# Last attention of a four-block transformer kernel: the fifth maximum ahead of four halves of output weights, the fifth scores half a column block later

## The chip, the cores and the metric

The kernel runs on one core of a Trainium2 chip. The time is that of the device for one launch, in microseconds. The kernel before has a median of 1317.13 us in three runs (1316.91 to 1317.64).

## The reference

One sequence of 256 tokens, width 1024, float32 throughout, passes through four blocks and two final norms: stick-breaking attention with an MLP, retention with an MLP, gated linear attention with a convolutional FFN, and, last, a sparse attention (NSA) with an FFN. The change lies in this last attention. Cut to it:

```
kv = (rmsnorm(x, g_kv) @ w_kv)                  # keys and values of three branches, 4 heads of 64
k_cmp, v_cmp = compress(kv[0]), compress(kv[1])  # 15 blocks of 32 tokens, a small MLP with gelu
q     = (rmsnorm(x, g) @ w_in)[:, :1024]         # 16 heads of 64;  gates = sigmoid(the last 48 columns)
p_cmp = masked_softmax(q @ k_cmp.T * scale);  o_cmp = p_cmp @ v_cmp
q_rot = rope(q)
o_sel = masked_softmax(q_rot @ k_sel.T * scale) @ v_sel
o_win = masked_softmax(q_rot @ k_win.T * scale) @ v_win
x     = x + (gates[0]*o_cmp + gates[1]*o_sel + gates[2]*o_win) @ w_o
```

With 256 tokens every block is selected, so the two uncompressed branches are plain causal attention.

## The kernel before

All 212 weight pieces of 128 x 2048 pass through one pipeline, each in two halves of 128 x 1024. SyncE loads a half into a ring of four raw buffers (`stream`), ScalarE rounds it to w_hi (`hi_half`, L1352), VectorE takes the rest as w_lo (`lo_half`, L1938), and TensorE multiplies with three products, hi·hi, hi·lo and lo·hi (`mm3`, L592 to L594). The raw buffer of half q comes free when VectorE has done half q - 4:

```
                if turn is not None or q >= RAW:
                    sp.wait_ge(lo_ready, plus(q - RAW + 1, turn, RAW))
```

w_hi and w_lo hold four pieces each; `refill(g)` on ScalarE waits for TensorE to be done with piece g and then copies both halves of piece g + 4. The halves come in the same order on every engine. So the DMAs of the two halves of piece G_NSA+16 wait for VectorE's two halves of G_NSA+14.

The order on each engine is that of the code, and every engine works its instructions in that order; between the engines stand semaphores. The last attention begins at piece G_NSA = 161. Its queries come in column blocks of 256 (`transposed`: two parts j of 128 columns, eight k of three matmuls each), pieces G_NSA+6 and G_NSA+11 to G_NSA+13. Into these blocks other steps are put: `mid` between the two parts, `late` ahead of k = 4 of the second. The output weights are pieces G_NSA+14 to G_NSA+17.

The attention has 16 steps `it`, two for each pair of heads (selected and window branch). For each: scores on TensorE (`ns_qk`, L1210), mask and maximum on VectorE (`ns_scores`, L2545), exponential on ScalarE (`ns_exp`, L1795), coefficient on VectorE (`ns_coef`, L2556 and L2561), the multiplication on GpSimd (L534), transposes on TensorE (`ns_t`, L1223), copies, and the product with the values (`ns_pv`, L1235 and L1241), whose result ScalarE copies (`ns_hi`, L1812 and L1814) and VectorE splits (`ns_lo`, L2565). ns_qk(it) waits for the maximum of the step before. "The fifth scores" are ns_qk(4).

The compressed branch comes in two parts c: `ns_cmp_kv` (L1163, L1168), `ns_cmp_values` (L2505), scores on TensorE (`ns_cmp_qk`, L1181), which wait for the maximum 5 + c, `ns_cmp_scores` on VectorE (L2518 to L2522), `ns_cmp_exp` on ScalarE (L1784), `ns_cmp_p` on VectorE (L2529 to L2533), the transpose on TensorE (`ns_cmp_t`, L1190), which is the `late` step of the column block G_NSA+13. Queries are scaled by `ns_queries` (L1985) when their block is done, swapped by a matmul (`ns_swap`, L1133) and rotated by `ns_rope` (L2460, L2467) and, on GpSimd, L526.

What ScalarE does around the change, in its order:

```
            ns_cmp_keys()
            ns_exp(4)
            refill(G_NSA + 12)
            ns_cmp_exp(0)
            ns_exp(5)
            ns_cmp_copy(0)
            ns_hi(0)
            ns_cmp_exp(1)
            ns_hi(1)
            ns_copy(4)
```

Here refill(G_NSA + 12) copies both halves of piece G_NSA+16. ns_t(4) on TensorE waits, by nsa_o_copied, for the first copy of ns_hi(1).

Of the kernel before, what the change touches and what calls it, by code (L numbers as in the profile page):

```python
# [72 lines left out]
G_NSA = 161  # L73
# [6 lines left out]
def build(nc, ws, small, narrow, tables, decay, rows, x_in, out):  # L80
    from contextlib import ExitStack
    ctx = ExitStack()
    with ctx:
# [461 lines left out]
        def _(pe):  # L545
# [25 lines left out]
            def x_tiles(n, k, t=1):  # L571
                if k % 2 == 0:
                    pe.wait_ge(xT_lo, xt_at(n, t, k // 2))
# [12 lines left out]
            def split(g, e):  # L586

                pe.wait_ge(lo_ready, 2 * g + e + 1)

            def mm3(o, lh, ll, rh, rl, start, stop):  # L590

                mm(o, lh, rh, start=start, stop=False, skip_group_check=True)  # L592
                mm(o, lh, rl, start=False, stop=False, skip_group_check=True)  # L593
                return mm(o, ll, rh, start=False, stop=stop, skip_group_check=True)  # L594

            def transposed(g, b, first=None, mid=None, src=(x_hi, x_lo), late=None):

                s = g % RING
                for j in range(2):
                    if j == 1 and mid is not None:  # L600
                        mid()
                    for k in range(KT):
                        if (j, k) == (1, 4) and late is not None:
                            late()
                        if j == 0 and k % 4 == 0:
                            split(g, k // 4)
                        if first is not None and j == 0:
                            x_tiles(first, k)
                        c = k * 256 + j * P
                        r = mm3(ps[:, b, j * T:(j + 1) * T], w_hi[:, s, c:c + P], w_lo[:, s, c:c + P],  # L610
                                src[0][:, k, :], src[1][:, k, :], k == 0, k == KT - 1)
                r.then_inc(done, 1)
# [511 lines left out]
            mixed = (y_hi, y_lo)  # L1124

            def ns_swap(i):

                if i < 2:
                    pe.wait_ge(nsa_kv, 3 + i)
                else:  # L1130
                    pe.wait_ge(nsa_q_in, i - 1)
                b, src = (4 + i, ns_k[:, i, :, :]) if i < 2 else (i % 2, ns_q[:, 2 * (i - 2):2 * (i - 2) + 2, :])
                mm(ps[:, b, :], swap, src, start=True, stop=True).then_inc(nsa_swapped, 1)  # L1133
# [25 lines left out]
            def ns_cmp_kv():  # L1159

                pe.wait_ge(nsa_gelu, 3)
                for c in range(2):
                    r = mm(ps[:, 2, 384:448], sm[:, S_W2K + c * P:S_W2K + (c + 1) * P], ns_h[:, 2, c, :],  # L1163
                           start=c == 0, stop=c == 1)
                r.then_inc(nsa_cmp_kv, 1)
                for g in range(2):
                    for c in range(2):
                        r = mm(ps[:, 3, 384 + g * 64:384 + (g + 1) * 64], ns_hv[:, g, c, :],  # L1168
                               sm[:, S_W2V + c * 64:S_W2V + (c + 1) * 64], start=c == 0, stop=c == 1)
                r.then_inc(nsa_cmp_kv, 1)  # L1170
# [22 lines left out]
            def ns_qk(it):  # L1193


                pr, br = it // 2, it % 2
                if it < 2:
                    pe.wait_ge(nsa_kd_other, it + 1)
                    pe.wait_ge(nsa_sin, 2)
                if it >= 5:  # L1200
                    pe.wait_ge(nsa_cmp_scores_copied, 1 if it < 6 else 2)
                if it >= 6:
                    pe.wait_ge(nsa_cmp_pT_copied, 1 if it < 10 else 2)
                pe.wait_ge(nsa_roped, pr // 2 + 1)
                if it:
                    pe.wait_ge(nsa_max, it)
                for t in range(TT):
                    for i in range(2):
                        v = slice(64 * i, 64 * i + 64)
                        r = mm(ps[:, 4 + i, P * t:P * (2 * t + 1)], ns_qr[v, pr, t * P:(t + 1) * P],  # L1210
                               ns_kd[v, br, pr // 2, 0:P * (t + 1)], start=t == 0, stop=True, skip_group_check=True)
                r.then_inc(nsa_scores, 1)

            def ns_t(it):
                pe.wait_ge(nsa_p, it + 1)
                if it:
                    pe.wait_ge(nsa_pT_copied, it)
                    pe.wait_ge(nsa_pT_copied2, it)
                if it >= 4:
                    pe.wait_ge(nsa_o_copied, 2 * max(it // 2, 2) - 1)  # L1220
                for i in range(2):
                    for j in range(3):
                        r = nc.tensor.transpose(ps[:, 6 + i, j * P:(j + 1) * P],  # L1223
                                                ns_s[it][:, i, j * P:(j + 1) * P], ident)
                r.then_inc(nsa_pT, 1)
# [64 lines left out]
            pe.wait_ge(nsa_gate_in, 1)  # L1290
            transposed(G_NSA + 11, 1, src=mixed, mid=lambda: (ns_hidden_t(), ns_t(2)))
            ns_t(3)
            transposed(G_NSA + 12, 0, src=mixed, mid=lambda: (ns_swap(3), ns_cmp_kv(), ns_qk(4)))
            ns_cmp_qk(0)
            ns_swap(4)
            ns_qk(5)
# [624 lines left out]
        def _(dve):  # L1921
# [13 lines left out]
            def lo_half(q):  # L1935
                g, v = q // 2, slice((q % 2) * HALF, (q % 2 + 1) * HALF)
                dve.wait_ge(hi_ready, q + 1)
                V.tensor_tensor(w_lo[:, g % RING, v], ring[:, q % RAW, :], w_hi[:, g % RING, v].bitcast(F32),  # L1938
                                ALU.subtract).then_inc(lo_ready, 1)

            def lo(g):
                lo_half(2 * g)
                lo_half(2 * g + 1)

            def refill(g):
                if g + RING < G_END:
                    lo(g + RING)
# [285 lines left out]
            for u in range(8):  # L2233
                dve.wait_ge(small_in, RET_SMALL + u + 1)
                b, src = rt_pair[u % 4][0], rt_small[:, u % 2, :].rearrange("p (a t) -> p a t", t=T)
# [198 lines left out]
            late = ffn(0)  # L2434
# [15 lines left out]
            def ns_queries(u):  # L2450
                dve.wait_ge(done, G_NSA + (7 if u == 0 else 11 + u))
                scaled(ns_q[:, 2 * u:2 * u + 2, :], ps[:, u % 2, :], scale, 0.125).then_inc(nsa_q_in, 1)
# [3 lines left out]
            def ns_sin(i):  # L2456
                dve.wait_ge(nsa_swapped, i + 1)
                if i >= 2:
                    dve.wait_ge(nsa_roped, i - 2)
                V.tensor_tensor(ns_t2[i == 1], ps[:, 4 + i if i < 2 else i % 2, :].rearrange("p (a t) -> p a t", t=T), rsin,  # L2460
                                ALU.mult).then_inc(nsa_sin, 1)
# [7 lines left out]
            def ns_rope(u):  # L2469
                ns_sin(2 + u)  # L2470
                ns_roped(u)
# [42 lines left out]
            def ns_cmp_scores(c):  # L2514
                s, m, _ = ns_cmp(c)
                dve.wait_ge(nsa_cmp_scores, c + 1)
                add = tab[:, C_CADD:C_CADD + TT * CMP].rearrange("p (t n) -> p t n", n=CMP)
                V.tensor_tensor(s, ns_cmp_at.rearrange("p t (h n) -> p t h n", n=CMP),  # L2518
                                add.unsqueeze(2).broadcast_to([P, TT, 8, CMP]), ALU.add).then_inc(nsa_cmp_scores_copied, 1)
                dve.wait_ge(nsa_cmp_scores_copied, c + 1)  # L2520
                link(V.tensor_reduce(m, s, AX.X, ALU.max))
                V.tensor_tensor(s, s, m.unsqueeze(3).broadcast_to([P, TT, 8, CMP]), ALU.subtract).then_inc(nsa_cmp_shifted, 1)  # L2522
# [27 lines left out]
            def ns_coef(it):  # L2550

                dve.wait_ge(nsa_exp, it + 1)
                if it >= 4:
                    dve.wait_ge(nsa_p, it - 3)
                l, f = ns_l[:, it % 4, :, :], ns_f[:, it % 4, :, :]
                link(V.reciprocal(f, l))  # L2556
                pr, br = it // 2, it % 2
                if it == 0:
                    dve.wait_ge(nsa_gate_in, 1)
                g = ns_gate[:, :, 16 * (br + 1) + 2 * pr:16 * (br + 1) + 2 * pr + 2].rearrange("p t h -> p h t")  # L2560
                V.tensor_tensor(f, f, g, ALU.mult).then_inc(nsa_coef, 1)  # L2561
# [64 lines left out]
            ns_gelu()  # L2626
            ns_copy(3)
            ns_rope(1)
            refill(G_NSA + 10)
            ns_cmp_values()  # L2630
            ns_scores(4)
            lo_half(2 * (G_NSA + 15))
            ns_queries(2)
            ns_cmp_scores(0)
            ns_coef(4)
            ns_scores(5)
            ns_cmp_p(0)
            ns_rope(2)
            ns_coef(5)
            lo_half(2 * (G_NSA + 15) + 1)  # L2640
            ns_queries(3)
            lo_half(2 * (G_NSA + 16))
            ns_lo(0)
            ns_sin(5)
            ns_cmp_scores(1)
            ns_scores(6)
            ns_lo(1)
# [244 lines left out]
```

## Time and profile before

| | |
|---|---|
| median of three runs | 1317.13 us |
| profiled execution: time | 1316.63 us |
| profiled execution: span | 1314.9 us |
| TensorE busy | 1305.7 us, 99% of the span |
| VectorE busy | 981.3 us, 75% |
| ScalarE busy | 758.8 us, 58% |
| GpSimd busy | 125.4 us, 10% |
| granted clock of TensorE, mean | 0.999 |

The profile comes from one execution. Its times are counted from the span's start. The engines' names in it are PE (TensorE), DVE (VectorE), ACT (ScalarE), POOL (GpSimd) and SP (SyncE). A row of a timeline gives start, duration, engine, line and operation; in square brackets stands how long the engine was idle ahead of it and which instruction ended that. Instructions of an engine overlap a little, so that one can start about 0.1 us before the one ahead of it ends, and matmuls overlap by more.

### The profile page before, as it was taken

How to read it: one execution, taken by the hardware profiler on the slowest of the kernel's cores; microseconds unless marked ns; L12 is line 12 of the kernel's file. 1: busy time of each engine (PE TensorE's matmuls, PEld its weight loads, DVE VectorE, ACT ScalarE, POOL GpSimd, SP SyncE). 2: the span in 40 equal slices, each digit the busy share in tenths (PEclk: the TensorE clock that was granted, in tenths of full speed). 3: DMA queues.
4: the chain of work that ended last, by engine and by line, in shares of the span. 5: the costliest groups of instructions: out<-in, count | busy, mean ns of one | idle time of the engine just before them, and what ended most of it. 6: DMA issues, size and time to landing. Idle time of an engine off the chain costs nothing.

```text
span 1314.9 us, 20491 instructions
## 1 busy us (share of the span) xinstructions
PE 1305.7 (99%) x7401; PEld 1118.4 (85%) x7401; DVE 981.3 (75%) x1518; ACT 758.8 (58%) x1231; POOL 125.4 (10%) x123
## 2 busy tenths in 40 slices
PE   9999999999999999999999999999999999999998
PEld 8888888888888888888889888888889878888886
DVE  5957765657846657665668768998868986899886
ACT  6655554536445446454566357666658756766663
POOL 0101000001600100000001310000003234000000
PEclk9999999999999999999999999999999999999999
DMA  7536656565654465656555445565546422466651
GB/s 263 194 129 207 224 186 206 175 205 163 198 194 133 155 225 159 223 172 210 170 162 201 128 162 170 192 207 189 190 155 210 139 71 81 161 192 196 200 193 53
DMA packets 64022, 231.61 MB, mean 176 GB/s; under 512 B 7104, under 2 KB 7488, under 8 KB 63936
## 3 DMA queue, kind: packets, MB, share of 16 engines
q1 hardware_dynamic: 62208, 224.42, 52.3%
q10 hardware_dynamic: 1728, 6.00, 1.3%
q8 instruction: 59, 0.97, 0.3%
q14 instruction: 27, 0.22, 0.1%
HBM read 229.34 MB, written 1.05 MB: 175 GB/s over the span
## 4 chain that ended last, share of the span: by engine, by line
PE 97%; DVE 2%; issue 1%; ACT 0%; POOL 0%; POOLq 0%; DVEq 0%
PE ps L645 25%; PE ps L592 17%; PE ps L594 17%; PE ps L593 17%; PE ps L653 13%; PE ps L564 1%; PE ps L1049 1%; PE ps L1241 1%; PE ps L1223 1%; PE ps L1210 1%; DVE w_lo L1938 1%; PE ps L884 0%; PE ps L873 0%; PE ps L1133 0%; PE ps L1235 0%
## 5 line engine op out<-in xcount | busy, mean ns | idle before, releaser
L1938 DVE TENSOR_TENSOR w_lo<-ring,w_hi 128x1024 fp32r<-128x1024 f32 x423 | 518.5, 1257 | 127.5 <-ACT w_hi L1352 126.9
L1352 ACT ACTIVATE w_hi<-ring 128x1024 fp32r<-128x1024 f32 x423 | 431.4, 1054 | 145.0 <-PE ps L594 116.3
L645 PE MATMUL ps<-x_both,w_hi 128*128 128x512 f32 x1408 | 340.1, 392 | 0.0
L645 PEld LDWEIGHTS ps<-x_both,w_hi 128*128 128x128 f32 x1408 | 258.5, 188 | 52.7 <-issue 1.6
L592 PE MATMUL ps<-w_hi,y_hi 128*128 128x512 f32 (+1 forms) x564 | 221.1, 392 | 0.0
L593 PE MATMUL ps<-w_lo,y_hi 128*128 128x512 f32 (+1 forms) x564 | 219.0, 388 | 0.0
L594 PE MATMUL ps<-w_hi,y_lo 128*128 128x512 f32 (+1 forms) x564 | 218.9, 388 | 0.0
L653 PEld LDWEIGHTS ps<-x_both,w_lo 128*128 128x128 f32 x1408 | 182.1, 191 | 7.9
L653 PE MATMUL ps<-x_both,w_lo 128*128 128x256 f32 x1408 | 184.5, 283 | 0.0
L594 PEld LDWEIGHTS ps<-w_hi,y_lo 128*128 128x128 f32 x564 | 105.9, 188 | 22.2
L592 PEld LDWEIGHTS ps<-w_hi,y_hi 128*128 128x128 f32 x564 | 106.1, 188 | 21.5 <-issue 0.8
L593 PEld LDWEIGHTS ps<-w_lo,y_hi 128*128 128x128 f32 x564 | 106.1, 188 | 19.9
L592 PE MATMUL ps<-w_hi,x_both 128*128 128x512 f32 (+1 forms) x300 | 118.6, 395 | 0.4 <-DVE w_lo L1938 0.4
L594 PE MATMUL ps<-w_hi,x_both 128*128 128x512 f32 (+1 forms) x300 | 113.8, 379 | 0.0
L593 PE MATMUL ps<-w_lo,x_both 128*128 128x512 f32 (+1 forms) x300 | 113.4, 378 | 0.0
L438 POOL TENSOR_TENSOR stat<-stat,power 128x1 f32<-128x1 f32 x20 | 10.9, 547 | 853.0 <-DVE stat L1933 675.6
L1458 ACT ACTIVATE arena<-arena,sm 128x256 f32<-128x256 f32 x88 | 48.2, 595 | 38.3 <-DVE arena L2095 38.3
L1374 ACT ACTIVATE x_both<-ps,sm 128x128 fp32r<-128x128 f32 x128 | 35.8, 374 | 59.1 <-PE ps L564 59.0
L592 PEld LDWEIGHTS ps<-w_hi,x_both 128*128 128x128 f32 (+1 forms) x300 | 54.6, 182 | 14.0 <-issue 4.0
L594 PEld LDWEIGHTS ps<-w_hi,x_both 128*128 128x128 f32 (+1 forms) x300 | 54.5, 182 | 11.0
L593 PEld LDWEIGHTS ps<-w_lo,x_both 128*128 128x128 f32 (+1 forms) x300 | 54.7, 182 | 9.7 <-issue 0.5
L592 PE MATMUL ps<-x_both,w_hi 128*128 128x256 f32 x192 | 55.0, 286 | 0.0
(262 smaller groups left out, 1521.9 us busy)
## 6 DMA issues: line engine op xcount, KB each, us to landing
ring<-ws SPq DMA_DIRECT2D x424, 512.0 KB, 4.8
tab<-tables ACTq DMA_DIRECT2D x3, 572.0 KB, 5.8
rowg<-rows ACTq DMA_DIRECT2D x3, 512.0 KB, 6.4
h<-x SPq DMA_DIRECT2D x4, 256.0 KB, 6.1
arena<-decay ACTq DMA_DIRECT2D x1, 768.0 KB, 10.1
sm<-small ACTq DMA_DIRECT2D x1, 642.0 KB, 6.4
arena<-narrow ACTq DMA_DIRECT2D x1, 512.0 KB, 6.7
out<-arena SPq DMA_DIRECT2D x2, 256.0 KB, 2.2
```

What stands on the lines that cost most here:

```text
L564: r = nc.tensor.transpose(ps[:, base + k // 2, t * T + (k % 2) * P:t * T + (k % 2 + 1) * P], h[:, t, k * P:(k + 1) * P], ident)
L592: mm(o, lh, rh, start=start, stop=False, skip_group_check=True)
L593: mm(o, lh, rl, start=False, stop=False, skip_group_check=True)
L594: return mm(o, ll, rh, start=False, stop=stop, skip_group_check=True)
L645: mm(ps[:, b + j, :], w_hi[:, s, c:c + P], x_both[:, k, :, :], start=k == 0, stop=False, skip_group_check=True)
L653: r = mm(ps[:, b + j, T:2 * T], w_lo[:, s, c:c + P], x_hi[:, k, :], start=False, stop=k == KT - 1, skip_group_check=True)
L1049: r = mm(o, keys, q, start=True, stop=True, skip_group_check=True)
L1210: r = mm(ps[:, 4 + i, P * t:P * (2 * t + 1)], ns_qr[v, pr, t * P:(t + 1) * P], ns_kd[v, br, pr // 2, 0:P * (t + 1)], start=t == 0, stop=Tr ...
L1352: A(w_hi[:, q // 2 % RING, c:c + HALF], ring[:, q % RAW, :], ACT.Copy).then_inc(hi_ready, 1)
L1374: r = A(dst[:, k, t * P:(t + 1) * P], ps[:, base + b, t * T + (k % 2) * P:t * T + (k % 2 + 1) * P], ACT.Copy, scale=gain(n, k))
L1458: r = A(conv[:, u % 2, e, :], conv_in[:, u % 2, e, :], ACT.Identity, scale=par(u, 4 + e), bias=par(u, 6 + e))
L1938: V.tensor_tensor(w_lo[:, g % RING, v], ring[:, q % RAW, :], w_hi[:, g % RING, v].bitcast(F32), ALU.subtract).then_inc(lo_ready, 1)
```

## The change

On VectorE the two halves of piece G_NSA+14 (until now refill(G_NSA + 10)) leave their place ahead of ns_cmp_values; they stand on either side of ns_cmp_scores(0). The two halves of G_NSA+15 and the first of G_NSA+16 move back likewise. On TensorE ns_qk(4) moves from `mid` to `late` of the column block G_NSA+12. ScalarE, GpSimd and SyncE keep their order.

```diff
-            transposed(G_NSA + 12, 0, src=mixed, mid=lambda: (ns_swap(3), ns_cmp_kv(), ns_qk(4)))
+            transposed(G_NSA + 12, 0, src=mixed, mid=lambda: (ns_swap(3), ns_cmp_kv()), late=lambda: ns_qk(4))
...
             ns_rope(1)
-            refill(G_NSA + 10)
             ns_cmp_values()
             ns_scores(4)
-            lo_half(2 * (G_NSA + 15))
             ns_queries(2)
+            lo_half(2 * (G_NSA + 14))
             ns_cmp_scores(0)
+            lo_half(2 * (G_NSA + 14) + 1)
             ns_coef(4)
             ns_scores(5)
             ns_cmp_p(0)
             ns_rope(2)
             ns_coef(5)
+            lo_half(2 * (G_NSA + 15))
+            ns_queries(3)
             lo_half(2 * (G_NSA + 15) + 1)
-            ns_queries(3)
-            lo_half(2 * (G_NSA + 16))
             ns_lo(0)
             ns_sin(5)
+            lo_half(2 * (G_NSA + 16))
             ns_cmp_scores(1)
```

VectorE from the end of ns_rope(1) (L2467) on, before: L1938 are halves of weights, L2505 ns_cmp_values, L2545 on arena<-ps,tab the fifth maximum.

```order
 L2467 TENSOR_TENSOR arena<-arena 128x512
-L1938 TENSOR_TENSOR w_lo<-ring,w_hi 128x1024 x2
 L2505 TENSOR_TENSOR arena<-ps,tab 128x512 x2
 L2545 ISA arena<-ps,tab 128x128
```

The two halves ahead of the maximum are gone from there. Right behind the maximum, up to the coefficient of the fifth step (L2556), VectorE changes as follows; L1985 is ns_queries(2), L2518 to L2522 ns_cmp_scores(0).

```order
-L1938 TENSOR_TENSOR w_lo<-ring,w_hi 128x1024
-L1985 SCALAR_TENSOR_TENSOR arena<-ps,arena 128x512
+L1985 SCALAR_TENSOR_TENSOR arena<-ps,arena 128x512
+L1938 TENSOR_TENSOR w_lo<-ring,w_hi 128x1024
 L2518 TENSOR_TENSOR arena<-ps,tab 128x2x128
 L2521 TENSOR_REDUCE arena<-arena 128x2x8
 L2522 TENSOR_TENSOR arena<-arena 128x2x128
+L1938 TENSOR_TENSOR w_lo<-ring,w_hi 128x1024
 L2556 RECIPROCAL arena<-arena 128x4
```

Where one half of G_NSA+15 stood, there are now the two of G_NSA+14, one ahead of the compressed scores and one behind them. Ahead of the second part of the compressed scores, a half stands between ns_sin(5) (L2460) and ns_cmp_scores(1) that stood ahead of ns_lo(0) (L2565) before.

```order
 L2460 TENSOR_TENSOR arena<-ps,tab 128x512
+L1938 TENSOR_TENSOR w_lo<-ring,w_hi 128x1024
 L2518 TENSOR_TENSOR arena<-ps,tab 128x2x128
 L2521 TENSOR_REDUCE arena<-arena 128x2x8
 L2522 TENSOR_TENSOR arena<-arena 128x2x128
```

The halves ahead of this point are the same five as before.

## Rows read from the trace of the kernel before

**Rows 1.** The page's first part: busy us, share, instructions.

```profile
PE 1305.7 (99%) x7401; PEld 1118.4 (85%) x7401; DVE 981.3 (75%) x1518; ACT 758.8 (58%) x1231; POOL 125.4 (10%) x123
```

**Rows 2.** Timeline of TensorE: start, us, instruction, idle before.

```profile
1048.40 0.93 PE L1210 MATMUL ps<-arena 64*128 64x128 f32 x8 [0.22 <-DVE arena L2467]
1049.26 0.39 PE L592 MATMUL ps<-y_hi,w_hi 128*128 128x256 f32 x1
...
1052.11 0.28 PE L594 MATMUL ps<-y_hi,w_lo 128*128 128x256 f32 x1
1053.07 1.94 PE L1181 MATMUL ps<-arena 128*128 128x32 f32 x16 [0.68 <-DVE arena L2545]
...
1055.88 0.93 PE L1210 MATMUL ps<-arena 64*128 64x128 f32 x8
...
1061.15 0.38 PE L1190 MATMUL ps<-sm,arena 128*128 128x128 f32 x2
...
1069.55 0.93 PE L1210 MATMUL ps<-arena 64*128 64x128 f32 x8
1070.40 0.87 PE L1223 MATMUL ps<-sm,arena 128*128 128x128 f32 x6
```

**Rows 3.** Timeline of VectorE, 1048 to 1076.

```profile
1048.27 2.35 DVE L1938 TENSOR_TENSOR w_lo<-ring,w_hi 128x1024 fp32r<-128x1024 f32 x2
...
1051.74 0.28 DVE L2545 CUSTOM_DVE_ANT_0 arena<-ps,tab 128x128 f32<-128x128 f32 x1
...
1052.84 0.08 DVE L2545 DVE_READ_ACCUMULATOR2_ANT arena<- 128x1 f32 x1
...
1053.98 0.68 DVE L1985 SCALAR_TENSOR_TENSOR arena<-ps,arena 128x512 f32<-128x512 f32 x1
1055.05 0.42 DVE L2518 TENSOR_TENSOR arena<-ps,tab 128x256 f32<-128x256 f32 x1 [0.39 <-PE ps L1181]
...
1060.24 0.68 DVE L2460 TENSOR_TENSOR arena<-ps,tab 128x512 f32<-128x512 f32 x1
...
1061.86 1.22 DVE L1938 TENSOR_TENSOR w_lo<-ring,w_hi 128x1024 fp32r<-128x1024 f32 x1
...
1063.61 2.02 DVE L1938 TENSOR_TENSOR w_lo<-ring,w_hi 128x1024 fp32r<-128x1024 f32 x1
...
1067.66 0.42 DVE L2518 TENSOR_TENSOR arena<-ps,tab 128x256 f32<-128x256 f32 x1
...
1073.99 0.41 DVE L2529 TENSOR_REDUCE arena<-arena 128x16 f32<-128x256 f32 x1
...
1075.14 0.42 DVE L2533 TENSOR_TENSOR arena<-arena 128x256 f32<-128x256 f32 x1
```

**Rows 4.** Timeline of ScalarE, 1054 to 1070.

```profile
1054.73 1.99 ACT L1352 ACTIVATE w_hi<-ring 128x1024 fp32r<-128x1024 f32 x2
...
1069.04 0.42 ACT L1784 ACTIVATE arena<-arena 128x256 f32<-128x256 f32 x1 [3.29 <-DVE arena L2522]
1069.66 0.38 ACT L1812 ACTIVATE arena<-ps 128x256 f32<-128x256 f32 x1 [0.21 <-PE ps L1241]
```

**Rows 5.** DMAs into the ring, 1049 to 1053; last row: 1063 to 1068.

```profile
L403 SPq DMA_DIRECT2D ring<-ws x2: 333/333/333, 1049.7 to 1050.8; - x2
...
DMA to landing us min/median/max: 3.7/4.3/4.8
...
DMA to landing us min/median/max: 3.5/3.6/3.7
```

**Rows 6.** Timeline of GpSimd, 1062.

```profile
1062.02 2.52 POOL L534 TENSOR_TENSOR arena<-arena 128x256 f32<-128x256 f32 x2 [2.39 <-DVE arena L2561]
```

**Rows 7.** Windows: TensorE busy, granted clock, DMA share, GB/s.

```profile
1308.00:1309.00 1.00, 0.46 (x4) 1.00 0.11 43
...
1311.00:1312.00 1.00, 0.00 (x0) 1.00 0.00 0
1312.00:1313.00 1.00, 0.00 (x0) 0.56 0.40 144
```

## The prediction

> **What bounds the kernel now.** I read the page first. Its busy line has TensorE occupied for 99% of the span [rows 1], so the kernel is one long file of matmuls and time is lost or won only where that file stops. I then asked for the waits of TensorE in the last attention (1015 to 1105 us) and found three short ones; the timeline of TensorE shows the two that the change touches [rows 2]. The fifth scores, ns_qk(4) at L1210, start at 1048.40 after 0.22 us of idleness, released by VectorE's rotated queries. The first compressed scores, ns_cmp_qk(0) at L1181, start at 1053.07 after 0.68 us, released by the fifth maximum (L2545). Third, the timeline of VectorE says why that maximum is late: two halves of output weights (L1938 x2, 2.35 us at 1048.27) stand ahead of it, so ns_scores(4) runs only from 1051.74 to 1052.92 [rows 3]. Fourth, and this decides for me, ScalarE: its two weight copies of piece G_NSA+16 (L1352 x2 at 1054.73) stand directly ahead of the exponential of the compressed scores (L1784), and they find their data already there [rows 4]. That data comes by DMAs which SyncE may issue only when VectorE has finished the two halves of G_NSA+14, because lo_ready frees the raw buffer four halves on. In the kernel before they were issued at 1049.7 and 1050.8 and landed 3.7 to 4.8 us later [rows 5], by about 1055.6, just as ScalarE came to the second.
>
> **The change, step by step.** All times are the profiled execution's, with span 1314.9 and time 1316.63 us against the median of 1317.13; the two differ by 0.5 us, so I add a difference worked out here to the median. Nothing is added or removed in work: the same 12 x 2 matmuls, the same five half subtractions; all is order.
>
> *Fifth scores.* The column block's second half resumes when ns_cmp_kv ends, about 1048.1 (0.22 us of idleness before 1048.40). Its 24 matmuls started from 1049.26 to 1052.11, 23 steps in 2.85 us: 0.12 us each and 0.1 once for the restart behind another operation. So twelve with a restart take 1.54 us [rows 2]. ns_qk(4) now starts at 1049.65 (no wait: the rotated queries were ready at 1048.3) and ends 0.93 later, 1050.58; the matmul behind it can start after 0.86 (1048.40 to 1049.26). VectorE has had only ns_cmp_values, 1.1 us, since 1048.3 and stands idle. From its start to TensorE's release the maximum took 1053.07 - 1051.74 = 1.33 us [rows 2, 3]: it starts at 1050.63, releases at 1051.96. TensorE itself needs 1049.65 + 0.86 + 1.54 = 1052.05. So ns_cmp_qk(0) starts at 1052.05, a **gain of 1.02 us**, and both waits are gone.
>
> *What is late next.* ns_queries(2) must wait for the column block's end (last matmul 1051.93 + 0.28) and holds VectorE for about 0.6 (0.68 with the overlap of the next instruction): until 1052.86. The first half of G_NSA+14 follows, 1.14 to the next start (of two in 2.35 us), and the compressed scores (TensorE until 1052.05 + 1.94 = 1053.99) are taken at 1054.04. From there to ScalarE's release took 1069.04 - 1067.66 = 1.38, so VectorE moves on after about 1.27: 1055.3. Only now comes the second half of G_NSA+14, 1.22 us, until **1056.52**; it was 1050.62. SyncE issues the DMA about 0.2 us later, 1056.7. Of landings the trace has 3.5 to 3.7 us for two DMAs 2.5 us apart, the spacing that these two now have, and 4.8 for one right behind another [rows 5]. I take 3.7 and keep 3.5 and 4.8: landed at 1060.4. ScalarE has been standing in its queue before that weight copy; behind it wait ns_cmp_exp(0), the exponentials of the sixth scores, and through them ns_cmp_p(0) on VectorE and ns_cmp_t(0) on TensorE. The copy takes about 0.95 to the next start, the exponential 0.40: VectorE gets it at 1061.82. ns_cmp_p ran 1.57 us where nothing disturbed it (1073.99 to 1075.56), TensorE reacts 0.15 later (1052.92 to 1053.07): **ns_cmp_t(0) at 1063.54**, where it stood at 1061.15. TensorE would be there at 1052.05 + 2.81 + 5.27 = 1060.13 (the stretches from 1053.07 over 1055.88 to 1061.15), so it idles some 3.2 us after the last matmul's 0.28, and the gain has become a **loss of 2.39 us**.
>
> *What follows.* TensorE can't make this up, having no wait to give back behind. VectorE is now late too: ns_cmp_p(0) lets ns_rope(2) start at 1063.32; in the trace it is 1.62 from there to the next half (1060.24 to 1061.86), then 1.75 with ns_queries(3) to the half after it (1061.86 to 1063.61): the last of the pair starts at 1066.69. From that half to ns_cmp_scores(1) it took 1067.66 - 1063.61 = 4.05; the change puts one more half between, 1.14 [rows 3]. So ns_cmp_scores(1) starts at 1071.88, its first instruction (0.42) and TensorE's reaction (0.15) release ns_qk(6) at 1072.45, against 1069.55 + 2.39 = 1071.94 by TensorE alone: the loss is 2.90. ScalarE then takes ns_cmp_exp(1) at 1071.88 + 1.38 = 1073.26 and behind it the copy of ns_hi(1) (L1812), 0.33 later (0.42 less the tenth by which its instructions overlap), 0.38 long; ns_t(4) on TensorE waits for that copy: 1073.97 + 0.15 = 1074.12, against 1070.40 [rows 2, 4]. The **loss is 3.7 us** when the steady part of the attention begins. The pieces from G_NSA+17 on are copied by ScalarE only in the rounds behind this point, the first in the round of pr = 3, so their DMAs, a few microseconds later too, are covered by two rounds of attention; without that cover each would cost what G_NSA+16 does.
>
> *Where the size is open.* The half at 1063.61 took 2.02 us, others 1.22, while GpSimd's two multiplications were running (2.52 us at 1062.02) [rows 3, 6]. If the two don't meet this time, the later steps shrink by up to 1.6 us, TensorE's own chain is the longer one and the loss stays at 2.4. I take the meeting, because GpSimd's multiplications are released by the same VectorE instructions in the same order as before. The Trainium skill (SBUF — State Buffer, section "SBUF: two separate sides") says that the port pair which these two engines share is an exclusive lock held for a whole instruction, and that the loser blocks fully. By that rule such a meeting is a matter of order and comes again, with the sum of 3.7; if the 0.8 us were only this execution's chance, the sum would be 2.4. With landings of 4.8 us the loss is 4.8, with 3.5 us and no meeting 2.2.
>
> **Rivals.** *The waits go and nothing takes their place* (not slower). Then TensorE keeps its 1.02 us: 1316.1. For it speaks that both waits shown on TensorE are really removed. It decides on one point: the second half of G_NSA+16 would have to land by about 1057.0 (1060.13 less 0.15, 1.57, 0.44 and 0.95), 0.3 us after its issue, and no landing of these rows is under 3.5 us. *VectorE and GpSimd don't meet*: the stall at ns_cmp_t(0) alone, 2.4 us: 1319.5. For it: the meeting depends on tenths. Against it: the order of both engines is unchanged there. *TensorE's clock falls in the stall.* After the last matmul of the kernel (ended 1308.46) the granted clock is still 1.00 in 1311 to 1312 and 0.56 on average in 1312 to 1313, so it fell in there from 2.4 to the lower level, 1.2 GHz [rows 7]. So it held full speed through 3.5 us of rest, and the new stall is 3.2: close. The cost would lie between nothing and the 8.4 us that TensorE works from ns_cmp_t(0) to ns_qk(6), doubled; nearest is the rest of the column block, 1.54 us, with a part of ns_pv(0): I take 2, so 1322.8. The Trainium skill (TensorE: Matmul & The Clock Gate, "Part 1: The HAM clock gate") has the clock fall to half once the engine has rested long enough; by that rule a slightly longer stall brings this case about.
>
> **How the numbers follow.** What a measurement of this kernel can tell is 0.2%, 2.6 us. Forecast (a loss of 3.7, itself 2.9 to 4.8): 62%. No meeting (2.0 to 2.8): 20%. Clock: 10%. No new wait: 3%. Something longer that I don't see: 5%. Median 1317.13 + 3.7 = **1320.8 us**. The range runs from 1318.8 (a loss of 1.7, a little under the 2.2 of the shortest landing without a meeting) to 1322.9 (5.8, with the clock's case at its middle); it leaves out the free gain and a fallen clock at its worst. Slower by over 0.2% has nearly all of the forecast, the clock's case, the unseen one and a quarter of the second: 0.78. Within 0.2%: most of the second rival, the gain of 1.0 us, which is too small to be told, and an edge of the forecast: 0.20. Faster: 0.02.
>
> **What would show it.** Right: in the waits of TensorE a new entry at L1190 of some 3 us, released by ns_cmp_p (L2533) at about 1063.5; in those of ScalarE, L1352 waiting for the DMA of ring for 4 to 6 us in two pieces; L1181 without a wait at about 1052; ns_t(4) released by ScalarE's L1812. Wrong in the mechanism: L1352 at G_NSA+16 without a wait for the DMA, or ns_cmp_exp(0) ahead of 1058. Wrong in size only: ns_cmp_t(0) late but ns_qk(6) at no more distance than it; or a clock under 1.00 in the slice behind the stall.

## The result, and the profile after

The changed kernel takes 1321.81 us in the median of seven runs (1321.35 to 1322.60), the kernel before 1317.13 us: a ratio of 1.0031, with a 95% interval of 1.0021 to 1.0041. By the ratio that is 4.1 us, by the medians 4.7. The span of the profiled execution is 1320.6 us against 1314.9. Of these 5.7 us, 1.17 lie ahead of the change: ns_swap(3) starts at 1047.05 instead of 1045.88, and the matmuls of 700 us were already as late; that is scatter, and other runs below show it too. From ns_swap(3) to ns_t(4) the kernel before takes 24.52 us, the changed one 29.08. These 4.56 us are what the change does, and all readings below count from ns_swap(3).

The waits of TensorE in the last attention: in total, times, longest.

```profile
PE ps L1190 <- DVE arena L2533: 4.2, 1, 4.2
PE ps L1223 <- POOL arena L534: 0.2, 1, 0.2
```

The waits at L1181 and L1210 are gone, as the change has it. In their place stands one of 4.2 us at ns_cmp_t(0). The timeline of TensorE, to be laid beside [rows 2]:

```profile
1047.05 1.02 PE L1133 MATMUL ps<-arena,tab 128*128 128x512 f32 x2
...
1050.77 0.93 PE L1210 MATMUL ps<-arena 64*128 64x128 f32 x8
...
1053.16 1.87 PE L1181 MATMUL ps<-arena 128*128 128x32 f32 x16
...
1055.90 0.93 PE L1210 MATMUL ps<-arena 64*128 64x128 f32 x8
...
1065.50 0.69 PE L1190 MATMUL ps<-sm,arena 128*128 128x128 f32 x2 [4.17 <-DVE arena L2533]
...
1075.28 0.93 PE L1210 MATMUL ps<-arena 64*128 64x128 f32 x8
1076.13 0.87 PE L1223 MATMUL ps<-sm,arena 128*128 128x128 f32 x6
```

ns_cmp_qk(0) comes 6.11 us after ns_swap(3), 1.08 earlier than before (7.19): the gain that was foreseen. ns_cmp_t(0) comes 18.45 us after it, against 15.27. VectorE, against [rows 3], and ScalarE, against [rows 4]:

```profile
1051.74 0.29 DVE L2545 CUSTOM_DVE_ANT_0 arena<-ps,tab 128x128 f32<-128x128 f32 x1 [1.02 <-PE ps L1210]
...
1056.35 1.22 DVE L1938 TENSOR_TENSOR w_lo<-ring,w_hi 128x1024 fp32r<-128x1024 f32 x1
...
1063.86 0.42 DVE L2529 TENSOR_REDUCE arena<-arena 128x16 f32<-128x256 f32 x1 [4.83 <-ACT arena L1784]
...
1068.73 0.69 DVE L1985 SCALAR_TENSOR_TENSOR arena<-ps,arena 128x512 f32<-128x512 f32 x1 [0.54 <-PE ps L594]
1069.34 1.40 DVE L1938 TENSOR_TENSOR w_lo<-ring,w_hi 128x1024 fp32r<-128x1024 f32 x1
1071.51 0.65 DVE L2565 TENSOR_TENSOR x_both<-arena,x_both 128x256 fp32r<-128x256 f32 x1 [0.77 <-ACT x_both L1814]
...
1073.82 0.41 DVE L2518 TENSOR_TENSOR arena<-ps,tab 128x256 f32<-128x256 f32 x1
```

```profile
1059.56 1.06 ACT L1352 ACTIVATE w_hi<-ring 128x1024 fp32r<-128x1024 f32 x1 [4.72 <-DMA ring<-ws]
1062.47 1.06 ACT L1352 ACTIVATE w_hi<-ring 128x1024 fp32r<-128x1024 f32 x1 [1.85 <-DMA ring<-ws]
1063.43 0.40 ACT L1784 ACTIVATE arena<-arena 128x256 f32<-128x256 f32 x1
...
1075.17 0.42 ACT L1784 ACTIVATE arena<-arena 128x256 f32<-128x256 f32 x1 [3.70 <-DVE arena L2522]
1075.49 0.36 ACT L1812 ACTIVATE arena<-ps 128x256 f32<-128x256 f32 x1
```

VectorE has idled 1.02 us ahead of the fifth maximum, and ends the second half of G_NSA+14 at 1057.57. It then waits 4.83 us for ScalarE's exponential (L2529 behind L1784). ScalarE waits 4.72 and 1.85 us in its two weight copies for the DMA of the raw ring. The second DMA, as the view of the ring shows it for 1057 to 1060 (in [rows 5] the same view):

```profile
L403 SPq DMA_DIRECT2D ring<-ws x1: 333/333/333, 1057.7 to 1057.7; - x1
...
DMA to landing us min/median/max: 4.7/4.7/4.7
```

Issued 0.16 us behind VectorE's half, landed 4.7 us later, at 1062.4, where ScalarE starts. One thing was given little weight beforehand: the granted clock. In these windows the columns are as in [rows 7]:

```profile
1064.00:1065.00 1.00, 0.00 (x0) 1.00 0.00 0
1065.00:1066.00 1.00, 0.50 (x3) 0.54 0.00 0
1066.00:1067.00 1.00, 1.00 (x6) 0.50 0.00 0
...
1068.00:1070.00 2.00, 2.00 (x26) 0.88 0.24 51
```

It falls at about 1065, toward the end of the wait, to the lower level, and is back by about 1068.5. (1.00 is 2.4 GHz, 0.50 is 1.2 GHz.) TensorE's last matmul before the wait had ended at 1061.33.

### The profile page after: what moved, and what is told of

Its sections match the earlier page's. It is cut to its first block, busy times and chain, and to the rows that moved or that the text cites. A ratio compares the mean times of both kernels' runs of the same rounds, so it can differ in the third digit from the quotient of the medians.

```text
span 1320.6 us, 20491 instructions
## 1 busy us (share of the span) xinstructions
PE 1308.2 (99%) x7401; PEld 1120.6 (85%) x7401; DVE 979.4 (74%) x1518; ACT 758.8 (57%) x1231; POOL 125.5 (10%) x123
## 4 chain that ended last, share of the span: by engine, by line
PE 97%; DVE 2%; issue 1%; ACT 0%; DMA 0%; POOL 0%; POOLq 0%; DVEq 0%; SPq 0%
PE ps L645 24%; PE ps L592 17%; PE ps L594 16%; PE ps L593 16%; PE ps L653 13%; PE ps L564 1%; PE ps L1049 1%; PE ps L1241 1%; PE ps L1223 1%; PE ps L1210 1%; DVE w_lo L1938 1%; PE ps L884 0%; PE ps L873 0%; DMA ring<-ws 0%; PE ps L1133 0%
## 5 line engine op out<-in xcount | busy, mean ns | idle before, releaser
L1938 DVE TENSOR_TENSOR w_lo<-ring,w_hi 128x1024 fp32r<-128x1024 f32 x423 | 517.8, 1255 | 130.5 <-ACT w_hi L1352 129.8
L1352 ACT ACTIVATE w_hi<-ring 128x1024 fp32r<-128x1024 f32 x423 | 431.5, 1054 | 155.8 <-PE ps L594 113.8
L594 PE MATMUL ps<-w_hi,y_lo 128*128 128x512 f32 (+1 forms) x564 | 218.9, 388 | 0.0
L594 PEld LDWEIGHTS ps<-w_hi,y_lo 128*128 128x128 f32 x564 | 105.9, 188 | 22.2
L594 PE MATMUL ps<-w_hi,x_both 128*128 128x512 f32 (+1 forms) x300 | 113.7, 379 | 0.0
L594 PEld LDWEIGHTS ps<-w_hi,x_both 128*128 128x128 f32 (+1 forms) x300 | 54.5, 182 | 11.0
```

Source lines behind the costliest of these rows:

```text
L1352: A(w_hi[:, q // 2 % RING, c:c + HALF], ring[:, q % RAW, :], ACT.Copy).then_inc(hi_ready, 1)
```

## Experiments

Each profile is one execution. The table has for each the time from ns_swap(3) (L1133) to ns_cmp_t(0) (L1190), from there to ns_t(4) (L1223), and their sum, and beside it the ratio of the timed runs to those of the kernel before with its 95% interval.

| kernel | swap to cmp_t | cmp_t to t(4) | sum | ratio |
|---|---|---|---|---|
| before | 15.27 | 9.25 | 24.52 | |
| changed | 18.45 | 10.63 | 29.08 | 1.0031 (1.0021 to 1.0041) |
| tensor_only | 16.82 | 9.25 | 26.07 | 1.0003 (0.9993 to 1.0012) |
| vector_only | 18.07 | 11.93 | 30.00 | 1.0035 (1.0022 to 1.0047) |
| scalar_order | 14.50 | 10.50 | 25.00 | 0.9998 (0.9989 to 1.0008) |
| scalar_order_before | 16.86 | 9.25 | 26.11 | 1.0004 (0.9995 to 1.0014) |
| halves_first | 16.07 | 10.50 | 26.57 | 1.0017 (1.0007 to 1.0027) |
| half_later | 19.57 | 11.56 | 31.13 | 1.0046 (1.0030 to 1.0063) |
| warm | 17.68 | 10.49 | 28.17 | 1.0026 (1.0015 to 1.0037) |
| cold_back | 18.14 | 10.84 | 28.98 | 1.0032 (1.0020 to 1.0044) |
| warm_back | 17.97 | 9.36 | 27.33 | 1.0021 (1.0011 to 1.0030) |
| both_orders | 14.50 | 9.36 | 23.86 | 0.9991 (0.9981 to 1.0001) |
| both_orders_again | 14.51 | 9.37 | 23.88 | 0.9992 (0.9983 to 1.0001) |

### Which part of the change: tensor_only and vector_only

```diff
# tensor_only: the kernel before with
-            transposed(G_NSA + 12, 0, src=mixed, mid=lambda: (ns_swap(3), ns_cmp_kv(), ns_qk(4)))
+            transposed(G_NSA + 12, 0, src=mixed, mid=lambda: (ns_swap(3), ns_cmp_kv()), late=lambda: ns_qk(4))
# vector_only: the changed kernel with this line as before
```

> The kernel before with TensorE's part of the change alone: ns_qk(4) half a column block later, VectorE as before. Theory (ScalarE's wait for the two late weight DMAs makes the loss): VectorE still works two weight halves until 1050.6 and takes the fifth maximum at 1051.74, so ns_qk(4) has 1 us of slack and TensorE only moves its wait; from ns_swap(3) to ns_t(4) the kernel before has 24.52 us, here 24.5 (24.2 to 24.8), total 1317 (ratio 1.000). Rival (the later scores cost something themselves): up to 0.9 us more, 25.4, total 1318.

> VectorE's part of the change alone: ns_qk(4) stays in the middle of the block. Theory: the second half of G_NSA+14 ends at about the same time as in the changed kernel (it waits for the compressed scores of TensorE), ns_cmp_t(0) waits 4 us again, the clock falls again; ns_swap(3) to ns_t(4) 29.1 to 29.4 us (changed kernel 29.08), total 1321.5 to 1322. Rival: the loss needs both parts, then under 27 us here.

VectorE's part alone makes the whole loss: ratio 1.0035, 30.00 us, a wait of 3.54 us at ns_cmp_t(0). The sum is over the 29.1 to 29.4 that was expected; the excess lies behind ns_cmp_t(0) and comes back below. TensorE's part alone measures no change, 1.0003, which the expectation had. But the sum in its profile is 26.07 and not 24.5, a miss that neither theory explains. The timeline of TensorE shows the new ns_qk(4) and a wait at L1181 that has grown to 0.93 us, since VectorE is as late as ever:

```profile
1045.77 1.02 PE L1133 MATMUL ps<-arena,tab 128*128 128x512 f32 x2
...
1049.48 0.93 PE L1210 MATMUL ps<-arena 64*128 64x128 f32 x8
...
1052.96 1.27 PE L1181 MATMUL ps<-arena 128*128 128x32 f32 x10 [0.93 <-DVE arena L2545]
...
1055.00:1056.00 1.00, 1.00 (x2) 0.65 0.76 127
1056.00:1058.00 2.00, 2.00 (x10) 0.50 0.53 197
```

L1181 comes 7.19 us after ns_swap(3), as before. What follows is slower, and the windows say why: the clock fell at about 1055.3, 2.3 us behind the end of that wait, and stayed down until about 1058.7. The time from ns_swap(3) to ns_t(4) is 1.55 us longer in this one execution. The timed runs have it in part: five of the ten list a mean granted clock of 0.998 and average 1318.7 us, the other five 0.999 and 1317.4. The kernel before has such executions too, 16 of 72 with 0.998, at 1318.4 against 1317.4, so the ratio stays at 1.0003.

### Is it the order of ScalarE's queue: scalar_order and scalar_order_before

```diff
# scalar_order: the changed kernel; scalar_order_before: the kernel before
             ns_exp(4)
-            refill(G_NSA + 12)
             ns_cmp_exp(0)
             ns_exp(5)
+            act.wait_ge(done, G_NSA + 13)
+            hi_half(2 * (G_NSA + 16))
             ns_cmp_copy(0)
+            hi_half(2 * (G_NSA + 16) + 1)
             ns_hi(0)
```

> The changed kernel, but ScalarE takes ns_cmp_exp(0) and ns_exp(5) ahead of the two weight copies of G_NSA+16, and ns_cmp_copy(0) between them. VectorE's and TensorE's orders are those of the change, the two DMAs are as late as there. Theory (it is the order of ScalarE's queue that turns the late DMAs into a wait of TensorE): ns_cmp_t(0) waits for nothing, the gain at ns_cmp_qk(0) is kept, ns_swap(3) to ns_t(4) takes 23.5 us (23.3 to 24.0), total 1316 (ratio 0.999). Rival (late weights or VectorE's own order make the loss): 27 us or more, 1320.

> The kernel before with ScalarE's new order alone. Theory: there the weights had landed when ScalarE came to them, so the order costs and gives nothing: ns_swap(3) to ns_t(4) 24.5 us (24.2 to 24.8), ratio 1.000. Rival (ScalarE's order is a gain by itself, and hid a loss of the change in the run with both): under 24 us.

The DMAs are as late as in the changed kernel (issued at 1054.0 and 1056.4, landed 4.0 and 4.2 us later), and yet ns_cmp_t(0) is there after 14.50 us instead of 18.45. So the late weights by themselves hurt nobody; what hurt was what stood behind them in ScalarE's queue. But the sum is 25.00 and not 23.5: of the two theories neither had the rest. TensorE in scalar_order:

```profile
1060.21 0.44 PE L1190 MATMUL ps<-sm,arena 128*128 128x128 f32 x2 [0.22 <-DVE arena L2535]
...
1068.99 0.93 PE L1210 MATMUL ps<-arena 64*128 64x128 f32 x8 [0.24 <-DVE arena L2520]
1070.71 0.52 PE L1223 MATMUL ps<-sm,arena 128*128 128x128 f32 x3 [0.80 <-ACT arena L1812]
```

ns_qk(6) waits for ns_cmp_scores(1) (L2520 in this file, L2518 where ScalarE's order is the old one), and ns_t(4) 0.80 us for the copy of ns_hi(1). These are the two later steps of the prediction, in their places, without any wait at ns_cmp_t(0) ahead of them; my expectation of 23.5 had forgotten them. The small wait at L1190 is new: ns_cmp_p(0) runs beside GpSimd's work, one of its instructions on 16 columns takes 1.14 us there (0.17 in the changed kernel, where GpSimd is idle at that moment), and TensorE is now early enough to notice. In the timed runs this kernel is no faster than the kernel before, 0.9998, where 0.999 was expected.

In scalar_order_before the order gives nothing (1.0004), as expected; its profile, at 26.11 us and so outside the expected 24.2 to 24.8, is off in the same way as that of tensor_only:

```profile
1053.38 1.94 PE L1181 MATMUL ps<-arena 128*128 128x32 f32 x16 [0.69 <-DVE arena L2547]
...
1063.04 0.38 PE L1190 MATMUL ps<-sm,arena 128*128 128x128 f32 x2
...
1055.00:1056.00 1.00, 1.00 (x5) 0.76 0.39 82
1056.00:1058.00 2.00, 2.00 (x10) 0.50 0.66 227
```

### One to one with the second half: halves_first and half_later

```diff
# halves_first
             ns_scores(4)
-            ns_queries(2)
             lo_half(2 * (G_NSA + 14))
-            ns_cmp_scores(0)
             lo_half(2 * (G_NSA + 14) + 1)
+            ns_queries(2)
+            ns_cmp_scores(0)
# half_later
             ns_cmp_scores(0)
-            lo_half(2 * (G_NSA + 14) + 1)
             ns_coef(4)
             ns_scores(5)
+            lo_half(2 * (G_NSA + 14) + 1)
```

> The changed kernel with both halves of G_NSA+14 directly behind the fifth maximum, ahead of ns_queries(2) and ns_cmp_scores(0): the second ends at 1055.2 on the changed kernel's scale instead of 1057.57. Theory (the wait at ns_cmp_t(0) follows the end of that half one to one, by DMA, weight copy and exponential): ns_cmp_t(0) 1.5 to 2.4 us earlier (the DMA is now close behind the other and lands later, 4.8 us), ns_swap(3) to ns_t(4) 26.7 to 27.6 us against 29.08, total about 1319.5. Rival (something else holds ns_cmp_exp(0), such as ns_cmp_scores(0) itself): no change, 29 us, or more since ns_cmp_scores(0) moves back.

> The changed kernel with the second half of G_NSA+14 behind ns_scores(5), 1.5 us later. Theory: one to one, ns_cmp_t(0) 1.5 us later, ns_swap(3) to ns_t(4) 30.6 us (30.0 to 31.2), total 1323.4. Rival (ns_cmp_exp(0) is held by something else): 29.1 us, 1321.8.

Counted from ns_swap(3), the second weight copy on ScalarE starts at 15.42 us in the changed kernel. In halves_first it starts at 13.03 (1059.83 less 1046.80), 2.39 earlier, and ns_cmp_t(0) comes 2.38 earlier. In half_later it starts at 16.53, 1.11 later, and ns_cmp_t(0) comes 1.12 later. ScalarE in these two:

```profile
1057.79 1.06 ACT L1352 ACTIVATE w_hi<-ring 128x1024 fp32r<-128x1024 f32 x1 [3.19 <-DMA ring<-ws]
1059.83 1.06 ACT L1352 ACTIVATE w_hi<-ring 128x1024 fp32r<-128x1024 f32 x1 [0.98 <-DMA ring<-ws]
```

```profile
1058.88 1.06 ACT L1352 ACTIVATE w_hi<-ring 128x1024 fp32r<-128x1024 f32 x1 [4.57 <-DMA ring<-ws]
1063.06 1.06 ACT L1352 ACTIVATE w_hi<-ring 128x1024 fp32r<-128x1024 f32 x1 [3.12 <-DMA ring<-ws]
```

And ns_cmp_t(0) in halves_first, then in half_later:

```profile
1062.87 0.44 PE L1190 MATMUL ps<-sm,arena 128*128 128x128 f32 x2 [0.76 <-DVE arena L2533]
```

```profile
1066.10 0.69 PE L1190 MATMUL ps<-sm,arena 128*128 128x128 f32 x2 [5.28 <-DVE arena L2533]
```

From the weight copy to ns_cmp_t(0) that is one to one, on both sides. The half itself ended 2.36 us earlier in halves_first, where the second DMA again took 4.7 us, and 1.92 us later in half_later, where it took 3.9: so from the half it is one to one as well, once the landing is counted. The sum of half_later, 31.13, falls into what was expected; that of halves_first, 26.57, lies 0.13 under its range of 26.7 to 27.6. In halves_first the sum is still 2.05 us over the kernel before, though ns_cmp_t(0) is only 0.80 late: the rest is again 10.50 instead of 9.25.

### The clock, and the half ahead of ns_cmp_scores(1): warm, cold_back, warm_back

```diff
# warm: four matmuls in the wait; bank 2 is free there, and nothing reads them
-            transposed(G_NSA + 13, 1, src=mixed, late=lambda: ns_cmp_t(0))
+            transposed(G_NSA + 13, 1, src=mixed, late=lambda: (keep_clock(4, 2), ns_cmp_t(0)))
# cold_back: the changed kernel, warm_back: warm, both with
-            lo_half(2 * (G_NSA + 16))
             ns_cmp_scores(1)
+            lo_half(2 * (G_NSA + 16))
```

> The changed kernel with four matmuls of 128x512 in float32 into a free bank ahead of ns_cmp_t(0), some 3.5 us of work inside the wait of 4.2 us; their result is used by nothing. The granted clock should then stay at 1.00. Theory A (VectorE and ScalarE are late by as much behind the wait: ns_cmp_scores(1) at the same time, then ns_cmp_exp(1) and the copy of ns_hi(1)): the fallen clock is hidden, ns_swap(3) to ns_t(4) 28.9 us (28.6 to 29.1) against 29.08. Theory B (the fallen clock is what made cmp_t to t(4) longer by 1.4 us): 27.7 us, total 1320.4.

> The changed kernel with the first half of G_NSA+16 behind ns_cmp_scores(1) on VectorE, nothing else. Behind the wait at ns_cmp_t(0) two causes are each able to make ns_cmp_t(0) to ns_t(4) 1.3 us longer than the 9.25 before: the fallen clock and this half. Theory (they lie beside each other, the longer counts): taking the half away alone gives nothing, 10.5 to 10.65 us, total as the changed kernel, 1321.5. Rival (the half is the only cause): 9.3 us, total 1320.4.

> The same with the four matmuls in the wait, so that the clock stays at 1.00. Theory: only now does it fall to 9.3 to 9.4 us, total 1.2 us under the run with the matmuls alone (1321.1), 1319.9. Rival (GpSimd's part or the earlier landing sets it): still 10.5 us.

With the matmuls in the wait (L552, which the trace lists as eight) the granted clock is 1.00 throughout. TensorE in warm and in warm_back:

```profile
1060.71 3.59 PE L552 MATMUL ps<-sm 128*128 128x512 f32 x8
1064.27 0.44 PE L1190 MATMUL ps<-sm,arena 128*128 128x128 f32 x2
...
1073.04 0.93 PE L1210 MATMUL ps<-arena 64*128 64x128 f32 x8 [0.24 <-DVE arena L2518]
1074.76 0.41 PE L1223 MATMUL ps<-sm,arena 128*128 128x128 f32 x2 [0.80 <-ACT arena L1812]
```

```profile
1064.47 0.44 PE L1190 MATMUL ps<-sm,arena 128*128 128x128 f32 x2 [0.26 <-DVE arena L2533]
...
1072.92 0.93 PE L1210 MATMUL ps<-arena 64*128 64x128 f32 x8
1073.83 0.85 PE L1223 MATMUL ps<-sm,arena 128*128 128x128 f32 x6
```

Four runs make a square, with one profile each. From ns_cmp_t(0) to ns_t(4) it takes 10.63 us with the fallen clock and the half (changed), 10.49 with the half alone (warm), 10.84 with the fallen clock alone (cold_back), 9.36 with neither (warm_back), 9.25 before. So either cause makes the stretch more than a microsecond longer, and both together cost no more than one: they lie beside each other, the clock on TensorE's own path, the half on that over VectorE and ScalarE. Taking away the clock alone, or the half alone, gives 0.14 and nothing. That was theory A of warm for this stretch. The 10.84 of cold_back is a little over the expected 10.5 to 10.65 and over the changed kernel's 10.63: its clock fell only at about 1065.5, when TensorE was already at work again, and not within the wait. The sum of warm missed its 28.9 all the same, at 28.17: 0.77 of the difference stands ahead of ns_cmp_t(0), where the second DMA landed after 3.9 us and not 4.7. The timed runs have the same order, 1.0026 for warm and 1.0021 for warm_back against 1.0031 and 1.0032, but these intervals overlap. By the ratios warm gains some 0.7 us over the changed kernel, more than the 0.14 of this stretch; whether its DMA lands earlier in every execution isn't known, so it stays open how much of that is the clock.

The two may also not be equal. Where the clock fell earlier in the wait, it was also down longer, and it cost more than the half. In vector_only it was down from about 1062.8 to 1069.6, twice as long as in the changed kernel, and the stretch took 11.93 us; in half_later from about 1064.3 to 1071.1, and it took 11.56. The windows of vector_only:

```profile
1062.00:1064.00 2.00, 0.12 (x1) 0.71 0.00 0
1064.00:1066.00 2.00, 2.00 (x10) 0.50 0.00 0
...
1068.00:1070.00 2.00, 2.00 (x24) 0.59 0.71 242
```

### A version that keeps the gain: both_orders

```diff
# scalar_order, and on VectorE
-            lo_half(2 * (G_NSA + 16))
             ns_cmp_scores(1)
+            lo_half(2 * (G_NSA + 16))
```

> The kernel with ScalarE's new order (ns_cmp_exp(0) and ns_exp(5) ahead of the weight copies), and the first half of G_NSA+16 behind ns_cmp_scores(1) on VectorE instead of ahead of it. Theory (the second term of the prediction: that half delays ns_cmp_scores(1), ns_cmp_exp(1) and the copy of ns_hi(1) behind it, and through them ns_qk(6) and ns_t(4)): ns_cmp_t(0) to ns_t(4) returns from 10.5 to 9.25 us, as in the kernel before; ns_swap(3) to ns_t(4) 23.8 us against 24.52 before and 25.00 with ScalarE's order alone; total 1316.7 (ratio 0.9995), both waits at L1210 and L1223 gone. Rival (it is the earlier ns_cmp_t(0) that meets a bound of its own there, such as GpSimd): still 10 us or more.

> The same kernel as both_orders, in more rounds: ScalarE's exponentials ahead of the weight copies, and the first half of G_NSA+16 behind ns_cmp_scores(1). Theory: 0.7 us faster than before in an undisturbed execution and, since the wait at L1181 is gone behind which the clock fell in two of the profiles, without the executions of before that are a microsecond longer: ratio 0.9992 to 0.9995, with the upper end of its interval near 1. Rival: it is the same as before, 1.0000.

```profile
1047.51 1.02 PE L1133 MATMUL ps<-arena,tab 128*128 128x512 f32 x2
...
1062.01 0.44 PE L1190 MATMUL ps<-sm,arena 128*128 128x128 f32 x2 [0.21 <-DVE arena L2535]
...
1070.45 0.93 PE L1210 MATMUL ps<-arena 64*128 64x128 f32 x8
1071.37 0.84 PE L1223 MATMUL ps<-sm,arena 128*128 128x128 f32 x6
```

The stretch behind ns_cmp_t(0) takes 9.36 us as soon as the half stands behind ns_cmp_scores(1), the waits at L1210 and L1223 are gone, and the sum is 23.86 and 23.88 us, 0.65 under the kernel before. The medians are 1316.42 against 1317.54 us and 1316.66 against 1317.64. Both intervals end at 1.0001, so each of the two leaves no change just possible, and their agreement is what speaks for a gain of about a microsecond. Of the 72 executions of the kernel before, those with a mean clock of 0.999 average 1317.4 us, and the 21 of both_orders and both_orders_again 1316.6: some 0.8 us of the gain is there without the clock.

## Why the prediction was right

**The mechanism** was the predicted one, step by step. ns_cmp_qk(0) gained 1.08 us (1.02 foreseen). The second half of G_NSA+14 ended 10.52 us behind ns_swap(3) (10.64 foreseen), and the DMA, the weight copy, ns_cmp_exp(0), ns_cmp_p(0) and ns_cmp_t(0) followed in a chain; scalar_order shows that ScalarE's queue is the link, halves_first and half_later that it passes delays on one to one.

**The first term** was sized at 2.39 us and measured 3.18 in the profile. The step that was off is the landing: I took 3.7 us, it was 4.7, near the 4.8 that I kept for the range. ScalarE's two waits add up to 6.57 us for it, over the 4 to 6 that I named. In the other profiles with these two DMAs some 2.4 us apart it was 3.9 to 4.7. The choice by spacing, from two landings, was too sure.

**The second term**, from 2.39 to 3.7, was 1.33 us; measured are 1.38 in the changed kernel, and 1.24 where only its cause was at work (warm). Its mechanism was right, the half ahead of ns_cmp_scores(1) and the order of ns_cmp_exp(1) and ns_hi(1) on ScalarE: ns_t(4) waits for L1812 in scalar_order, warm and halves_first, 0.80 us each time. But in the changed kernel itself it is not what TensorE waits for. There the fallen clock takes the same time on TensorE's path and a tenth more, so the sign that I named, ns_t(4) released by ScalarE, did not appear.

**The meeting of VectorE and GpSimd** came only in part. ns_cmp_scores(1) came 26.77 us behind ns_swap(3), against 26.00 foreseen: late by 0.77, as ns_cmp_t(0) was by 0.79. But two departures cancel in between. ns_queries(3) waited 0.54 us for the column block (L594), which ran at the lower clock, so the half behind it started 2.37 us after the one ahead instead of 1.75. And from that half to ns_cmp_scores(1) it took 4.48 us instead of 5.19, since the half took 1.40 us and not 2.02 and the split behind it (L2565) 0.65 and not 1.26. In warm, with the clock up, the meeting came whole: the half took 2.03 us, the split 1.48, and the same distance was 5.09. No run takes the meeting away alone, so what it is worth was not shown.

**The clock** was a rival with 10%, of which I argued that 3.2 us of rest were less than the 3.5 through which it held at the kernel's end. That argument failed. The wait was longer, 4.17 us, and in vector_only, with 3.54, the clock was down some 2.5 us after the last matmul. The price of 2 us is near what the fallen clock cost by itself, 1.59 us in cold_back (10.84 against 9.25) and 2.68 in vector_only, where the half lies beside it. But I had it on top of the rest, and in the changed kernel it lies beside the second term, where warm takes away 0.14 us. So a rival that I had given 10% came true, and the sum held because its cost was hidden: the two errors cancel, which is luck.

**The side with no loss** would have needed the second DMA to land within 0.3 us of its issue; the shortest landing of these two in any profile here was 3.7 us. Over the timed runs the loss is 4.1 us by the ratio, against 3.7; in the profile it is 4.56, and 0.79 of the excess of 0.84 stand in the first term.

## What to carry to other kernels

When work is moved back on one engine, follow what it frees, a raw buffer here, to the DMA that waits for it, and then read what stands behind that data's first reader in its queue: an engine that works in order turns a late transfer into a wait for everything behind it, whether it needs the data or not. Two causes that lie beside each other must both be taken away before either shows; a square of four runs tells them apart where single runs say "no effect". A profile of one execution carries a microsecond or two of scatter from elsewhere (ns_swap(3) started between 1045.7 and 1047.5 in the thirteen profiles), so count from an instruction just ahead of the change.

## What the runs showed that was not expected

The granted clock fell after much shorter rests than at the kernel's end. The long waits gave no fixed time either: it fell 2.5 us after the last matmul in vector_only, 3.5 in half_later, 3.7 in the changed kernel, and 4.7 in cold_back, where TensorE had been at work again for 0.9 us. In tensor_only the last rest was 0.93 us and in scalar_order_before 0.69, both at L1181; the clock went down 2.3 and 2.1 us after the wait's end, with TensorE at work again, at a price of 1.55 and 1.59 us. The kernel before had 0.68 us of rest at this place in its profile and kept its clock. So a rest of this length can go either way. That the rest is what brings the fall was not shown by a run that takes it away alone. The timed runs fit it: of the kernel before 16 of 72 executions list a mean clock of 0.998, of tensor_only and scalar_order_before 9 of 20, and of the kernels without the wait 1 of 10 (scalar_order) and none of 21 (both_orders, whose two profiles kept 1.00). The 16 are about a microsecond slower than the other 56, so their share in the gain of both_orders would be some 0.2 us. That is an estimate: the mean clock is rounded, and the profiled execution of halves_first lists 0.998 though its clock fell only behind the last matmul.

The Trainium skill (TensorE: Matmul & The Clock Gate, "Part 1: The HAM clock gate") ties the fall to rest; the four long waits here (3.5 to 5.3 us) agree, while the two short ones fell with most of the time before and behind them busy by the profile's account.

The landing of the second of these two DMAs, 512 KB issued some 2.4 us behind the other, varied from 3.9 us (warm) to 4.7 us (the changed kernel) between programs that differ in nothing ahead of it, and the time of ns_cmp_t(0) with it: 17.68 against 18.45 us. Why is open.
